# Strassen-Winograd products in the MLP down projections of a four-layer transformer kernel (one core of Trainium2)

## The reference, cut to what matters

```python
def sq_relu_mlp(h, w1, w2):
    a = jax.nn.relu(h @ w1)
    return (a * a) @ w2          # w1: 1024 x 4096, w2: 4096 x 1024

    a = rms_norm(h, norm_gains[layer, 2])
    h = h + rms_norm(sq_relu_mlp(a, mlp_w1[layer], mlp_w2[layer]), norm_gains[layer, 3])
```

## Time and profile before

| | us |
|---|---|
| median of three runs | 2552.24 (2552.04 to 2552.33) |
| the profiled execution: span from first to last instruction | 2550.6 |
| TensorE busy (matmul) | 2513.4 (99%) |
| GpSimd busy | 1669.3 (65%) |
| VectorE busy | 1074.4 (42%) |
| ScalarE busy | 685.0 (27%) |
| MLP of layer 0 | about 245 to 585 of the span |
| MLP of layer 1 | about 883 to 1213 of the span |

### The profile page before, as it was taken

How to read it: one execution, slowest core, us unless ns; L and a number is a source line. 1 busy time by engine, 2 the same in 40 slices (tenths; PEclk the granted TensorE clock), 3 DMA queues, 4 the chain that set the end, 5 groups by cost and what they waited for, 6 DMA issues and landing times.

```text
span 2550.6 us, 34483 instructions
## 1 busy us (share of the span) xinstructions
PE 2513.4 (99%) x12547; PEld 2054.6 (81%) x12547; DVE 1074.4 (42%) x1923; ACT 685.0 (27%) x1227; POOL 1669.3 (65%) x2118
## 2 busy tenths in 40 slices
PE   8999999999999999999989999999999999999999
PEld 6778888888787788888667888888888888888887
DVE  7444221127766411212785443435343343643432
ACT  3443111014645401101555211213112012411111
POOL 5355777776664677776662777677665755877774
PEclk9999999999999999999999999999999999999999
DMA  5122333233221232332220323233222322433231
GB/s 169 42 79 67 116 97 93 91 98 83 77 72 67 83 103 95 99 99 83 83 67 17 100 85 109 87 99 99 96 70 82 99 66 67 116 100 99 86 110 69
DMA packets 283924, 224.47 MB, mean 88 GB/s; under 512 B 13620, under 2 KB 271645, under 8 KB 283677
## 3 DMA queue, kind: packets, MB, share of 16 engines
q1 hardware_dynamic: 283148, 222.41, 28.9%
q10 hardware_dynamic: 656, 0.43, 0.1%
HBM read 220.72 MB, written 2.10 MB: 87 GB/s over the span
## 4 chain that ended last, share of the span: by engine, by line
PE 88%; DVE 7%; issue 2%; ACT 1%; DVEq 1%; DMA 0%; POOL 0%; ACTq 0%
PE proj L652 25%; PE proj L654 25%; PE proj L653 25%; PE proj L2635 1%; PE proj L2634 1%; PE proj L2633 1%; DVE top L2150 1%; DVEq L2153 1%; PE aux L2647 1%; PE proj L1041 1%; DVE acc L2088 1%; DVE aux L537 0%; DVE a_lo L739 0%; PE aux L1099 0%; PE proj L677 0%
## 5 line engine op out<-in xcount | busy, mean ns | idle before, releaser
L652 PE MATMUL proj<-a_hi,w_hi 128*128 128x512 f32 x1864 | 738.8, 396 | 0.0
L654 PE MATMUL proj<-a_hi,w_lo 128*128 128x512 f32 x1864 | 725.9, 389 | 0.0
L653 PE MATMUL proj<-a_lo,w_hi 128*128 128x512 f32 x1864 | 725.6, 389 | 0.0
L1606 POOL TENSOR_TENSOR pool_carrier<-small 128x1 f32<-128x1 f32 x441 | 100.8, 229 | 787.5 <-PE proj L654 672.5
L1629 POOL TENSOR_TENSOR w_lo<-raw,w_hi 128x512 fp32r<-128x512 f32 (+2 forms) x441 | 577.5, 1310 | 5.3
L1628 POOL TENSOR_TENSOR w_lo<-raw,w_hi 128x512 fp32r<-128x512 f32 x378 | 491.7, 1301 | 31.5
L652 PE MATMUL proj<-g_hi,w_hi 128*128 128x512 f32 x1104 | 431.6, 391 | 3.3 <-DVE g_lo L639 3.0
L654 PE MATMUL proj<-g_hi,w_lo 128*128 128x512 f32 x1104 | 429.6, 389 | 0.0
L653 PE MATMUL proj<-g_lo,w_hi 128*128 128x512 f32 x1104 | 429.5, 389 | 0.0
L652 PEld LDWEIGHTS proj<-a_hi,w_hi 128*128 128x128 f32 x1864 | 350.0, 188 | 80.7 <-issue 9.1
L653 PEld LDWEIGHTS proj<-a_lo,w_hi 128*128 128x128 f32 x1864 | 350.2, 188 | 73.8 <-issue 2.9
(11 more groups left out here) (375 smaller groups left out, 2687.9 us busy)
## 6 DMA issues: line engine op xcount, KB each, us to landing
raw<-in_mlp_w SPq DMA_DIRECT2D x64, 1024.0 KB, 5.6
raw<-in_f_w_up SPq DMA_DIRECT2D x88, 512.0 KB, 4.9
raw<-in_b_w_in SPq DMA_DIRECT2D x24, 1024.0 KB, 5.1
raw<-in_f_w_down SPq DMA_DIRECT2D x18, 1024.0 KB, 5.2
raw<-in_hgrn_w_in SPq DMA_DIRECT2D x32, 512.0 KB, 5.1
raw<-in_b_w_out SPq DMA_DIRECT2D x8, 1024.0 KB, 5.0
raw<-in_a_w_in SPq DMA_DIRECT2D x5, 1024.0 KB, 5.2
raw<-in_mla_w_o SPq DMA_DIRECT2D x4, 1024.0 KB, 5.2
```

The costliest lines, as they stand in the source:

```text
L652: pe.matmul(psum[r][:], w_hi[r][:, w], xh, start=k == 0, stop=False)
L653: pe.matmul(psum[r][:], w_hi[r][:, w], xl, start=False, stop=False)
L654: last = pe.matmul(psum[r][:], w_lo[r][:, w], xh, start=False, stop=k == kc - 1)
L1606: pool.tensor_tensor(pool_carrier[:], zero, zero, ALU.add)
```

## The change

**In turns 0 to 2 of both MLPs** (the "turns 1-3 of 4" of its description) the down product, 512 tokens x 1024 features x 1024 columns, is made of seven half-block products instead of eight. The activations A are cut into A11, A12, A21, A22 (256 tokens x 512 features), the rows of `w2` into B11, B12, B21, B22 (512 x 512), and product p multiplies one activation block or sum with one weight block or sum. Here the activations are the stationary operand (128 tokens) and the weights the moving one (512 columns): a product is 2 blocks of 128 tokens (b), each 4 chunks x 3 matmuls, 24 matmuls with 512 columns. The results stand by token; DVE sums them in `by_token`.

- **Weight sums.** B11 is loaded into the tile `chain` by SP, and GpSimd issues adding DMAs from HBM onto it: + B12 (product 2), + B22 (product 4), + B21 (product 6). Product 1 takes B21 from `raw`, product 3 B22, and product 5 B22 + B12, added onto `raw`. Each sum is two adding DMAs of half a MB (h = 0, 1), 8 in a turn, each issued when the half has been split for its last product.
- **Weight splits.** Each product fills two slots of the ring (1,024 elements a partition each): ACT rounds both halves, DVE subtracts half 0 in one pass of 1,024, GpSimd half 1 in two passes of 512. The slots come free when TensorE is done with product p - 2.
- **Activation sums.** Behind up units 0 to 3 DVE makes `g_lo` of the left half, the difference A11 - A21, and its `lo` (three passes of 256); behind up units 4 to 7 three sums of 256, and `lo` of 512, 512 and 256. The squares now lie in SBUF (`kept`, `second_square`), no longer in PSUM. ACT rounds each.
- **The last turn** runs as before, but its down units begin with the transposed sums: 4 transposes of 128 x 128 by TensorE in each of 8 column groups, on which the 24 matmuls add up.
- **The norm.** Relu of turn 0 waits for the finished factor; the sum of the norm moves into the middle of up unit 3.
- The loops over turns are written out. The three retention tables share memory with the new tiles and are loaded at the start of the sparse attention's output projection.

```diff
+    def free(self, p, h):
+        return self.done(self.at(p, h) - RING) if p < 2 else self.done(self.at(p - 2, 1))
+    def split(self, p):
+        return self.done(self.at(p, 1))
...
+        s4_hi, s4_lo = over("s4_hi", KS * HALF, ret_at), over("s4_lo", KS * HALF, F_at + 4 * 10 * T)
+        chain = F[:, 2 * T:6 * T]
+        by_token = F[:, 12 * T:20 * T]
+        kept = [tile(acc, k) for k in range(KS)]
...
+            def quarter(t, k, n):
+                return down[:, t * DC + k * KS:t * DC + (k + 1) * KS, n * T:(n + 1) * T]
+            sevens = []
+            for t in range(SEVENS):
+                quarters = [Slab(KS, units, lambda i, t=t, n=n: [(0, T, quarter(t, 1, n))], across=True) for n, units in ((0, 14), (1, 0))]
+                sevens.append(SevenStage(stages[-1], ups(t) + quarters, l * SEVENS + t, lambda k, n, t=t: quarter(t, k, n)))
+                stages.append(sevens[-1])
+            return sevens, stage(1, ups(SEVENS) + [plain(mlp_w2[l], k0=SEVENS * DC, col=lambda i, c=c: c * 256) for c in range(4)])
...
+            def seven_pe(self, pe, st, t):
+                for p in range(st.PRODUCTS):
+                    for b in range(2):
+                        if p in (0, 1):
+                            pe.wait_ge(bank_free[st.bank(st.at(p, b))], st.uses(st.at(p, b)))
+                        if p == 3:
+                            pe.wait_ge(*taken_sums(st, b))
+                        if p in (4, 5):
+                            pe.wait_ge(bank_free[st.bank(st.at(0, b))], st.uses(st.at(0, b)) + (1 if p == 4 else 2))
+                        o, begins = self.sum_bank(st, p, b), p in (0, 1, 2, 6)
+                        for k in range(KS):
+                            if b == 0:
+                                if k == 0:
+                                    pe.wait_ge(*w_low_at(st, p))
+                                if k == KS // 2:
+                                    pe.wait_ge(lo_split, st.split(p))
+                                pe.wait_ge(*self.x_low.at(self.rows_ready(p, k) if p < 2 else 5 * KS - 1, t))
+                            r, w = st.place(p, k // 2), slice(k % 2 * T, k % 2 * T + T)
+                            xh, xl = self.rows(p, k, b)
+                            pe.matmul(o[:], xh, w_hi[r][:, w], start=begins and k == 0, stop=False, skip_group_check=True)
+                            pe.matmul(o[:], xl, w_hi[r][:, w], start=False, stop=False, skip_group_check=True)
+                            last = pe.matmul(o[:], xh, w_lo[r][:, w], start=False, stop=k == KS - 1, skip_group_check=True)
+                        last.then_inc(unit_done, 1)
...
+            def turn_sums(pe, o, m, there):
+                for b in range(there.start // P, there.stop // P):
+                    at = b * D + m * P
+                    pe.matmul(o[:, b * P:b * P + P], by_token[:, at:at + P], ident[:], start=b == there.start // P, stop=False,
+                              is_transpose=True, skip_group_check=True)
...
+                def weights(st, p, h):
+                    r = st.place(p, h)
+                    act.wait_ge(*seven_in(st, p, h))
+                    act.wait_ge(unit_done, st.free(p, h))
+                    act.copy(w_hi[r][:], seven_raw(st, p)[:, h * 2 * T:(h + 1) * 2 * T]).then_inc(w_high, 1)
...
+                        k = j % KS
+                        emptied(act, st, j)
+                        if j >= KS + 2:
+                            act.wait_ge(*self.x_low.at(nth_s4(k - 2), t))
+                        dst = kept[j] if j < KS else second_square[j % 2]
+                        act.activation(dst, self.relu[j % 2], ACT.Square).then_inc(self.squared.sem, 1)
+                        act.wait_ge(*self.squared.at(j, t))
+                        if j < KS:
+                            act.copy(tile(g_hi, j)[:, self.LEFT], kept[j][:, self.LEFT]).then_inc(self.x_high.sem, 1)
+                            act.wait_ge(*self.x_sums.at(nth_sum3(k), t))
+                            act.copy(tile(g_hi, j)[:, self.RIGHT], kept[j][:, self.LEFT]).then_inc(self.x_high.sem, 1)
+                        else:
+                            act.copy(tile(g_hi, j), dst).then_inc(self.x_high.sem, 1)
+                            act.wait_ge(*self.x_sums.at(nth_sum2(k), t))
+                            act.copy(tile(s12_hi, k), s12[k % 2]).then_inc(self.x_high.sem, 1)
...
+                def weights(st, p):
+                    r = st.place(p, 0)
+                    dve.wait_ge(*w_high_at(st, p, 0))
+                    dve.tensor_tensor(w_lo[r][:], seven_raw(st, p)[:, 0:2 * T], w_hi[r][:].bitcast(F32),
+                                      ALU.subtract).then_inc(w_low, 1)
+                def first_rows(t, k):
+                    z = kept[k]
+                    dve.wait_ge(*self.x_high.at(nth_a11(k), t))
+                    dve.tensor_tensor(tile(g_lo, k)[:, self.LEFT], z[:, self.LEFT], tile(g_hi, k)[:, self.LEFT].bitcast(F32),
+                                      ALU.subtract).then_inc(self.x_low.sem, 1)
+                    dve.wait_ge(*self.x_low.at(nth_a11(k), t))
+                    dve.tensor_tensor(z[:, self.LEFT], z[:, self.LEFT], z[:, self.RIGHT],
+                                      ALU.subtract).then_inc(self.x_sums.sem, 1)
+                    dve.wait_ge(*self.x_high.at(nth_s3(k), t))
+                    dve.tensor_tensor(tile(g_lo, k)[:, self.RIGHT], z[:, self.LEFT], tile(g_hi, k)[:, self.RIGHT].bitcast(F32),
+                                      ALU.subtract).then_inc(self.x_low.sem, 1)
+                def second_rows(t, k):
+                    j, z, x, s = KS + k, kept[k], second_square[k % 2], s12[k % 2]
+                    dve.wait_ge(*self.squared.at(j, t))
+                    dve.tensor_tensor(s[:, self.LEFT], x[:, self.RIGHT], z[:, self.RIGHT], ALU.subtract).then_inc(self.x_sums.sem, 1)
+                    dve.scalar_tensor_tensor(s[:, self.RIGHT], z[:, self.LEFT], -1.0, x[:, self.RIGHT], ALU.mult,
+                                             ALU.subtract).then_inc(self.x_sums.sem, 1)
+                    dve.wait_ge(*self.x_sums.at(nth_sum2(k), t))
+                    dve.scalar_tensor_tensor(s4, x[:, self.LEFT], -1.0, s[:, self.RIGHT], ALU.mult,
+                                             ALU.subtract).then_inc(self.x_sums.sem, 1)
+                    dve.wait_ge(*self.x_high.at(nth_raw(k), t))
+                    dve.tensor_tensor(tile(g_lo, j), x, tile(g_hi, j).bitcast(F32), ALU.subtract).then_inc(self.x_low.sem, 1)
+                    dve.wait_ge(*self.x_high.at(nth_s12(k), t))
+                    dve.tensor_tensor(tile(s12_lo, k), s, tile(s12_hi, k).bitcast(F32), ALU.subtract).then_inc(self.x_low.sem, 1)
+                    dve.wait_ge(*self.x_high.at(nth_s4(k), t))
+                    dve.tensor_tensor(tile(s4_lo, k, HALF), s4, tile(s4_hi, k, HALF).bitcast(F32),
+                                      ALU.subtract).then_inc(self.x_low.sem, 1)
...
+            def first_quarter(st):
+                if st.number % SEVENS == 0:
+                    sp.wait_ge(*mlp[st.number // SEVENS].pre.high.at(0))
+                if st.number:
+                    sp.wait_ge(lo_split, st_seven[st.number - 1].split(6))
+                    sp.wait_ge(*w_low_at(st_seven[st.number - 1], 6))
+                sp.dma_start(chain.rearrange("p (k n) -> p k n", k=KS), st.quarter(0, 0)).then_inc(chain_in, 16)
...
+            def seven_low(st, p):
+                r = st.place(p, 1)
+                pool.wait_ge(*w_high_at(st, p, 1))
+                for n, passed in ((0, hi_split), (1, lo_split)):
+                    w = slice(n * T, (n + 1) * T)
+                    pool.tensor_tensor(w_lo[r][:, w], seven_raw(st, p)[:, 2 * T + n * T:2 * T + (n + 1) * T],
+                                       w_hi[r][:, w].bitcast(F32), ALU.subtract).then_inc(passed, 2)
+            def seven_add(st, p, k, n, signal, h):
+                if h:
+                    pool.wait_ge(lo_split, st.split(p))
+                else:
+                    pool.wait_ge(*w_low_at(st, p))
+                pool.dma_start(seven_raw(st, p)[:, h * 2 * T:(h + 1) * 2 * T].rearrange("p (k n) -> p k n", k=2),
+                               st.quarter(k, n)[:, 2 * h:2 * h + 2], accum_op=ALU.add).then_inc(signal[h], 16)
+            def seven_products(st):
+                seven_add(st, 0, 0, 1, chain_added, 0)
+                seven_low(st, 0)
+                seven_add(st, 0, 0, 1, chain_added, 1)
+                seven_low(st, 1)
+                seven_add(st, 2, 1, 1, chain_added, 0)
+                seven_low(st, 2)
+                seven_add(st, 2, 1, 1, chain_added, 1)
+                seven_add(st, 3, 0, 1, second_added, 0)
+                seven_low(st, 3)
+                seven_add(st, 3, 0, 1, second_added, 1)
+                seven_add(st, 4, 1, 0, chain_added, 0)
+                seven_low(st, 4)
+                seven_add(st, 4, 1, 0, chain_added, 1)
+                seven_low(st, 5)
```

(36 more changed lines are left out.)

272 lines of the change are left out of this document (193 added, 79 removed).

## The result

The changed kernel takes 2567.25 us, median of 4 runs (2564.83 to 2568.45), against 2552.23 us before in the same session (4 runs, 2552.04 to 2552.33): ratio 1.0057, 95% interval 1.0042 to 1.0071. It is slower, by 15 us. Forecast were 2564 and "slower" with 58%.

A forecast was written before the change was run, and what follows sets the result against it. TensorE, busy 2513 of 2550.6 us, was taken to bound the kernel. -32.6 + 8.3 + 2 x (0.7 + 11.4 + 2.9 + 2.9) + 2 x 0.4 = +12.3 gave 2564 us against the median, range 2538 to 2600.

The forecast's parts named there:

- case (e): Whole kernel: the forecast itself holds, 2564 us with its own range 2558 to 2574; chance 22%.
- (c): Adding DMAs: long issue (from 1.5 us) or slow landing (from 7) makes each product wait, 2580 to 2611; 28%.
- Removed matmuls: Down products of six turns: 7 x 24 matmuls instead of 8 x 24, at 0.227 us each, save 32.6 us.
- Transposes: Last turn's down units: 32 transposes a layer in 10 groups cost 4.1 us, +8.3 us for two layers.
- Norm: Up unit 3 of turn 0: TensorE waits 0.7 us for the norm's total, in each layer.
- Turn 0: Products 0 and 1 wait for weight halves, 3.1, 2.6, 3.5 and 2.2 us, together 11.4 us a layer.
- Turns 1 and 2: Product 1 waits 0.7 us at its start and 2.2 at its middle, 2.9 us a turn.
- the forecast's "1.0": Turns 1 and 2: product 0's half on GpSimd meets unit 6's sums and puts VectorE back by 1.0 us.
- Tables: Start of the kernel: the three tables leave a busy DMA queue, but TensorE does not wait there, so nothing gained.
- (a): VectorE and GpSimd: exclusion hardly bites, turn 0 loses 4.5 us, turns 1 and 2 0.3 each; 2540 us, 22%.
- (b): GpSimd's DMA issue takes only 0.43 us; turns 1 and 2 lose 1.2, turn 0 10.8; 2556.5 us, 20%.
- (d): GpSimd's DMA issue also waits for the VectorE pass it meets, up to 1.2 us; 2569.5 us, 8%.

The follow-up runs named there:

- experiment 1: Changed kernel with GpSimd's two passes for half 1 of each product writing one column instead of 512: 2544.8 us, ratio 0.9964 to the kernel before.
- experiment 9: Changed kernel with product 1's weight pass earlier, relu ahead in turn 0, contraction halves outermost, GpSimd's lower halves ahead of adding DMAs: 2544.8 us, 0.9965 of before.

## Why the prediction was right

The forecast was case (e), at 22% not the likeliest of its own list; (c), slower by more, had 28%. The mechanism was the one that it gave: products 0 and 1 wait, since VectorE and GpSimd shut each other out, and products 3, 4 and 6 do not. That 2564 lies so near to 2567 is in part luck, since errors of both signs cancelled: the waits of turn 0 came out 1.3 and 2.8 us below their 11.4, the transposes 0.9 below and the tables 1.4 below; turns 1 and 2 came out 0.45 to 0.8 above each, low clock in turn 0 of the two layers, which had no term, 2.5 and 2.2 above, and some 2 us outside the MLP as well. By its own steps:

- **Removed matmuls, -32.6.** Turn 2 of layer 1 takes 41.44 us from its first product to the next unit, of which 168 x 0.227 = 38.1 are work and 3.3 waits. Right.
- **Transposes, +8.3.** The down units of turn 3 start 5.93 us apart instead of 5.44; to the next stage layer 0 takes 3.7 us longer (48.30 for 44.58), layer 1 the same: 7.4.
- **Norm, 0.7.** 0.65 and 0.64.
- **Turn 0, 11.4.** 13.0 in layer 0 and 11.2 in layer 1 (end of unit 7 to the next turn, less 38.1). Of these 2.5 and 2.2 are low clock, which the sum had not, and some 0.4 each are steps a little above 0.227: the waits themselves were 10.1 and 8.6. Place by place, forecast 3.1, 2.6, 3.5 and 2.2, they were 2.4, 2.7, 3.6 and 1.4 in layer 0 and 2.6, 1.9, 2.1 and 1.95 in layer 1.
- **Turns 1 and 2, 2.9.** 3.7, 3.5, 3.35 and 3.35, of which 1.15 + 1.94 at product 1 (forecast 0.7 + 2.2). VectorE's sum was stretched by 2.4 us (2.85 for 0.42), but by experiment 1 it has 1.3 us to spare before unit 7, so that 1.05 arrive at product 1: the forecast's "1.0". GpSimd's issue cost 1.25 and not 1.0. The rest above 3.1, 0.25 to 0.6 a turn, is again in steps a little above 0.227.
- **Tables, "hidden at nothing".** Wrong in size: 1.4 us are gained at the start. VectorE comes 0.4 us earlier to a pass that met GpSimd's splits; the pass of 56.69 took 1.78 us and now, at 55.95, takes 1.09. No experiment undid the move alone, so whether this is due to the tables or to chance is open.
- **The sum.** -32.6 + 7.4 + 1.3 + 24.2 + 13.9 - 1.4 = +12.8, against +15.1 between the spans. Some 2 us lie outside the MLP, 1.4 of them between the end of layer 0 and the next stage's transposes; their cause is open.

Of the rivals, (a) falls by experiment 1, (b) by the issue of 1.20 us, (d) by issues beside VectorE's weight passes: that of 390.97 took 1.19 beside the pass of 390.82. The page *SBUF — State Buffer* of the Trainium skill ("Summary: rules for kernel authors") says that descriptor generation starves while VectorE is in its two-port modes. No row shows the mode of these passes, so this neither bears the rule out nor contradicts it. (c) holds in neither size, but its edge was near: 6.8 us of landing where it decides from 7, and experiment 9 ran into it. The page *Collectives: The Full Stack* of the Trainium skill ("The bandwidth ceiling: the fold count and why AG ≠ RS ≠ AR") says that an adding transfer runs at half the rate of a copy, since it reads two sources. The landing of 6.8 us against 3.8, each with whatever part of it is fixed, is 1.8 times as long and agrees; in the experiments that keep the adding transfers their median landing is 5.6 to 7.2 us, 1.5 to 1.9 times the plain one.

## What to carry to other kernels

A saving in the bounding engine's work is worth what the other engines' order lets through: here 32.6 us were saved and 38 lost in waits and the low clock behind them, nearly all of which belonged to the order of passes on engines half idle, and most of them came back without taking anything away. Look at who asks for a shared port just behind whom, and at each engine's queue where a new pass is put ahead of a pass that someone waits for. And price a wait of TensorE with the clock behind it: in turn 0 of layer 0 a wait of 3.6 us was followed by 2.5 of low clock.
